# Last head group of a layer in the instruction order of the others, in a hybrid attention encoder

## The reference, cut to what matters

```
for l in range(2):
    h = rms_norm(x, g)
    z = h @ w_in[l]                      # 1024 -> 4096: qd kd vd qn kn vn gate
    # differential attention, 4 heads with two score maps each
    p = softmax(qd @ kd.T / 8 - slope * |i - j|)
    o_da = rms_norm((p[0] - lam * p[1]) @ vd, subln_g) * (1 - lam_init)
    # 2-D neighbourhood attention, 8 heads: 16 rows x 64 columns of tokens,
    # each query sees 8 rows x 16 columns of keys
    p = softmax(qn @ kn_window.T / 8 + rpb, masked)
    o_na = p @ vn_window
    x = x + (concat(o_da, o_na) * silu(gate)) @ w_out[l]
return rms_norm(x, final_g)
```

## Time and profile before

| | us |
|---|---|
| median of 3 runs | 1439.88 |
| lowest, highest | 1439.75, 1440.21 |
| the profiled execution | 1440.11 |
| its span, first to last instruction | 1438.3 |
| TensorE busy in the span | 1417.8 |
| VectorE busy | 884.0 |
| ScalarE busy | 691.5 |
| GpSimd busy | 500.2 |

### The profile page before, as it was taken

How to read it: one execution, slowest core, us unless ns; L and a number is a source line. 1 busy time by engine, 2 the same in 40 slices (tenths; PEclk the granted TensorE clock), 3 DMA queues, 4 the chain that set the end, 5 groups by cost and what they waited for, 6 DMA issues and landing times.

```text
span 1438.3 us, 23719 instructions
## 1 busy us (share of the span) xinstructions
PE 1417.8 (99%) x8116; PEld 1153.9 (80%) x8116; DVE 884.0 (61%) x1827; ACT 691.5 (48%) x1373; POOL 500.2 (35%) x416
## 2 busy tenths in 40 slices
PE   9999999999999999999999999999999999999996
PEld 7788888887888888777887888788878888887875
DVE  7767677677556565653337777767676565656433
ACT  6545554555444444552515554545544444456231
POOL 3223223233333333443643231323233333337152
PEclk9999999999999999999999999999999999999998
DMA  5710101121211111301110110100202021213113
GB/s 183 154 30 29 45 22 36 36 62 38 62 38 55 45 48 49 128 30 59 58 44 30 38 37 15 44 29 22 77 23 65 36 62 36 63 38 125 45 59 117
DMA packets 40698, 79.57 MB, mean 55 GB/s; under 512 B 18992, under 2 KB 19248, under 8 KB 40624
## 3 DMA queue, kind: packets, MB, share of 16 engines
q1 hardware_dynamic: 40480, 78.60, 17.3%
q10 hardware_dynamic: 144, 0.01, 0.0%
HBM read 66.57 MB, written 15.96 MB: 57 GB/s over the span
## 4 chain that ended last, share of the span: by engine, by line
PE 93%; DVE 3%; ACT 2%; issue 1%; DMA 1%; SPq 0%; POOL 0%; POOLq 0%; DVEq 0%; ACTq 0%
PE proj L1045 19%; PE proj L1047 18%; PE proj L1046 18%; PE scores L1081 11%; PE turn L1138 6%; PE mix L1189 3%; PE mix L1190 3%; PE mix L1154 2%; PE mix L1156 2%; PE mix L1155 2%; PE scores L1138 2%; DVE pt_lo L1554 1%; PE mix L1164 1%; DMA xt<-x_t 1%; DVE cmix L1583 1%
## 5 line engine op out<-in xcount | busy, mean ns | idle before, releaser
L1045 PE MATMUL proj<-h_hi,w_hi 128*128 128x512 f32 x1184 | 490.8, 415 | 2.0 <-DVE h_lo L1445 0.5
L1047 PE MATMUL proj<-h_hi,w_lo 128*128 128x512 f32 x1184 | 465.2, 393 | 0.0
L1046 PE MATMUL proj<-h_lo,w_hi 128*128 128x512 f32 x1184 | 462.0, 390 | 0.0
L628 POOL TENSOR_TENSOR w_lo<-w_raw,w_hi 128x1024 fp32r<-128x1024 f32 x62 | 152.8, 2464 | 486.6 <-ACT w_hi L815 486.6
L1554 DVE TENSOR_TENSOR pt_lo<-turn,pt_hi 128x512 fp32r<-128x512 f32 x208 | 139.1, 669 | 225.6 <-ACT pt_hi L857 224.9
L1047 PEld LDWEIGHTS proj<-h_hi,w_lo 128*128 128x128 f32 x1184 | 222.2, 188 | 50.6
L1045 PEld LDWEIGHTS proj<-h_hi,w_hi 128*128 128x128 f32 x1184 | 223.0, 188 | 47.9 <-issue 10.5
L1046 PEld LDWEIGHTS proj<-h_lo,w_hi 128*128 128x128 f32 x1184 | 223.8, 189 | 35.0
L857 ACT ACTIVATE pt_hi<-turn 128x512 fp32r<-128x512 f32 x208 | 120.3, 578 | 225.4 <-PE turn L1138 225.1
L1546 DVE CUSTOM_DVE_ANT_0 prob<-scores,inner 128x1024 f32<-128x1024 f32 (+1 forms) x192 | 203.5, 1060 | 3.1 <-PE scores L1081 2.7
L882 ACT ACTIVATE prob<-prob,nm,escale_now 128x1024 f32<-128x1024 f32 x128 | 158.7, 1240 | 61.6 <-DVE nm L1550 61.1
(11 more groups left out here) (187 smaller groups left out, 2274.4 us busy)
## 6 DMA issues: line engine op xcount, KB each, us to landing
w_raw<-chunks SPq DMA_DIRECT2D x80, 512.0 KB, 3.5
mixed_dram<-gate SPq DMA_DIRECT2D x28, 256.0 KB, 2.2
edge<-bias_dram SPq DMA_DIRECT2D x32, 224.0 KB, 4.8
h_lo<-mixed_dram SPq DMA_DIRECT2D x14, 512.0 KB, 6.7
xt<-x_t SPq DMA_DIRECT2D x8, 512.0 KB, 8.5
out_t<-xt SPq DMA_DIRECT2D x16, 256.0 KB, 2.1
bias_dram<-bias_rows SPq DMA_DIRECT2D x16, 240.0 KB, 6.0
dist_dram<-inner SPq DMA_DIRECT2D x1, 480.0 KB, 6.2
```

The lines of the kernel that those rows point to most:

```text
L628: pool.tensor_tensor(w_lo[:, b], w_raw[:], f32(w_hi[:, b]), ALU.subtract).then_inc(w_lo_done, 1)
L1045: pe.matmul(dst, a_hi, b_hi, start=start, stop=False)
L1046: pe.matmul(dst, a_hi, b_lo, start=False, stop=False)
L1047: return pe.matmul(dst, a_lo, b_hi, start=False, stop=stop)
```

## The change

In the last group of each layer, the scores of tile t + 1 are now computed in step t, between the two transposed parts of tile t - 1 (`following` now also answers for the last group), instead of the scores of tile t at the start of step t. On VectorE the two passes over scores (`shifted`) go to the same place as in the other groups: behind the low parts and the reciprocal, ahead of the gate piece and of the additions of the step's last slot. On ScalarE the first exponentials of a tile stand ahead of the first high part of the step, the second exponentials ahead of the second high part. The reciprocal goes behind the first low part. The other groups, and GpSimd's and SyncE's lists, are as before.

```diff
         def following(g, behind, t):


-            if not g.project:
-                return None
-            return (g, t + 1) if t < NT - 1 else (behind, 0) if t == NT - 1 else None
+            if t < NT - 1:
+                return g, t + 1
+            return (behind, 0) if t == NT - 1 and behind else None
...
-                    elif t < NT and g.project:
+                    elif t < NT:
                         exponentials(front, ft, 0)
...
-                    p_first = t == NT or not g.project
+                    p_first = t == NT
...
-                if front and ft > 1 and not g.project:
-                    score(front, ft)
...
-                if front and ft > 1 and not g.project:
-                    shift_scores(front, ft)
...
-                    if c == 0 and front and t < NT and g.project:
+                    if c == 0 and front and t < NT:
                         combine(front, ft)
...
-                if front and (t == NT or not g.project):
+                if front and t == NT:
                     combine(front, ft)
```

## The result

| | before | after |
|---|---|---|
| median, runs | 1439.82, 4 | 1453.99, 4 |
| lowest, highest | 1439.39, 1440.21 | 1453.25, 1454.39 |
| ratio of after to before | | 1.0096, 95% interval 1.0084 to 1.0108 |
| the profiled execution | 1440.11 | 1454.24 |
| its span | 1438.3 | 1452.4 |

The account below looks back on a forecast made before the run. The prediction took TensorE, 93% of the chain of waits, as the bound. New waits of 7.2 us a layer less today's 1.8 make 5.4, +10.8 us in two layers: 1450.8 us, range 1445.5 to 1454.0.

Parts of the forecast that it names:

- C: Scores of step 5, step 4's weighing, row 5 and third transpose: new TensorE waits of 0.9 and 0.3 us a layer.
- D: Bank of the first output piece: VectorE's additions later, TensorE sooner; a wait of 2.7 us a layer, upper bound 3.0.
- gain at step 4: Scores between the transposes cover TensorE's 1.61 us wait; with step 2's 0.18, at best 1.8 us a layer won.
- A: Step 2's weighing: gate piece behind both passes delays the tanh and ScalarE's queue; a wait of 1.4 us a layer.
- B: Rows 1 and 2 for the output pieces come late through GpSimd: waits of 0.65 and 1.2 us, 1.9 a layer.
- rival 4: TensorE's clock falls to 1.2 GHz behind the longest new wait, 2.1 us more a layer: 1455.0; chance 0.04.
- Its other two signs: The forecast is also wrong if VectorE's `xt` releases no TensorE wait, or if ScalarE's first tanh stays near 596.
- rival 3: The output-piece bank wait is covered and only A to C bind, 2.7 us a layer: 1445.3; chance 0.08.
- Rival 1: The gap closes and nothing else gets late, the tanh not held: 1436.3; chance 0.05.
- rival 2: Only D binds, A to C hiding behind one another; 0.9 us a layer, with 0.3 left of C: 1442.3; chance 0.07.
- rival 5: The two orders cost the same, slacks being larger than the profile tells: within 0.2%; chance 0.04.
- the rule's own price: By the skill page's find-the-gaps rule alone, the result would be the gain of 1.8 us a layer: 1436.3.

Follow-up runs that it names:

- gate_first: Changed kernel with VectorE's gate pieces put back ahead of the passes over the next scores, additions as changed: 1449.07 us, ratio 1.0064 to the kernel before.
- adds_first: Changed kernel with VectorE's additions of output pieces 0, 1 and 2 back ahead of the passes over scores: 1449.63 us, ratio 1.0066 to the kernel before.
- before_gate_late: Kernel before, with only the last group's first gate piece moved behind VectorE's passes over step 2's scores: 1447.28 us, ratio 1.0053.
- before_adds_late: Kernel before, with only the additions of output pieces 0 and 1 moved behind VectorE's passes over step 6's scores: 1449.03 us, ratio 1.0063.
- both_hi_early: both_first plus ScalarE making output chunk 2's high part ahead of its copies of the weighed pair in step 6: 1441.33 us, ratio 1.0005 to the kernel before.
- before_s5: Kernel before, with only TensorE's scores of tile 5 put between the two transposes of step 4: 1439.56 us, ratio 0.9998.
- exp_as_before: Changed kernel with ScalarE's exponentials back in the order of before: 1458.39 us, ratio 1.0133 to the kernel before.
- both_first: Changed kernel with both gate pieces and additions ahead of VectorE's passes over scores: 1444.55 us, ratio 1.0028 to the kernel before.
- before_s5_both: before_s5 plus VectorE's passes over tile 5's scores at the end of step 4, ahead of its gate scaling: 1438.91 us, ratio 0.9991 to the kernel before.
- before_hi_early: Kernel before, with only ScalarE's high part of output chunk 2's weights ahead of its copies of the weighed pair in step 6: 1439.94 us, ratio 0.9996.
- before_s5_both_hi: Kernel before with the edits of both before_s5_both and before_hi_early: 1438.97 us, ratio 0.9989.

## Why the forecast came out as it did

The result is 3.2 us above the forecast, and the sign and the main mechanism were right. That it is still inside the range, by 0.01, is luck: the 3 us above the layout's 1450.8 were given to C and D at their upper bounds, and neither went there; what used them up are a wait that was left out and a fall of the clock. By its own steps, in layer 0, as read above:

| step of the forecast | forecast | measured |
|---|---|---|
| gain at step 4 (wait of 1.61 closes) | up to 1.8 with step 2 | 1.61 to 0.14 |
| A, weighing of step 2 | 1.4 | 1.43 |
| B, row 1 | 0.65 | 0.66 |
| B, row 2 | 1.2 | 1.29 |
| C, scores of tile 5 | 0.5 | 0.30 |
| C, weighing of step 4 | 0.4 | 0.14 |
| C, row 5 and the third transpose | 0.3 | 0.42 |
| D, bank of output piece 2 | 2.7 | 2.69 |
| E, weights of output chunk 2 | none | 1.44 |
| lower clock behind D, layer 1 alone | none, rival 4 | 1.43 |

- A, B and D were right in mechanism and size, and the experiments separate them: gate_first takes A and B away and leaves D, adds_first takes VectorE's part of D and leaves A and B, before_gate_late makes A alone (its list has no wait for `h_lo`) and before_adds_late makes VectorE's part of D alone. No run makes B alone; that it comes from the gate piece rests on gate_first.
- C was 0.34 too large in all: 0.86 where 1.2 was laid out. No run takes C away or makes it alone, so its three parts rest on the timeline.
- The step that failed is the sentence "Later steps have 6.9 us and more of matmuls and stay covered". It looked at when the row copies and additions were done, and left out the weights of output chunk 2. Moving the scores takes 1.3 us of TensorE's work, from start to start, from behind each weighing, and whatever hangs on the weighing through ScalarE and GpSimd gets that much less time. At step 6 there was no slack at all. The wait is 2.9 us in two layers, 0.2 of which were there before; both_hi_early measures 3.2.
- Rival 4, given 0.04, came in part: the clock fell behind the longest new wait in one layer of two, in the profiled run, for 1.4 us, less than the 2.1 a layer that it was priced at. The forecast had named this as a sign of being wrong ("if the granted clock falls in these waits"), and by that sign this part of it was: the layout held the clock at full speed. Its other two signs did not show: `xt` releases the largest wait, and the tanh starts at 598.01.
- In the numbers: 10.8 forecast, less 0.7 for C, plus 2.7 for E (1.44 less 0.11 a layer), plus 1.4 for the clock is 14.2; the two groups are 14.6 longer and the spans differ by 14.1.
- Two slips in the working are too small to matter. D's slack was taken as 0.24, where the bank was free at 624.24 and written at 624.53, 0.29. The range was said to reach down to rival 3, whose own time, 1445.3, lies below its end of 1445.5.
- Rivals 1, 2, 3 and 5 fall. Rival 1 rested on the old gap. It closes as that rival said, and before_s5 shows that this by itself is worth nothing that the time can tell: 0.9998. The Trainium skill's page "Perfetto Trace Analysis", "Optimization Strategy", advises to find the gaps and make what they depend on start sooner. before_s5 does the first half only: it fills the gap with other work, and the low part comes no sooner (25.55 where it was 25.53). No run here makes the low part itself earlier in the old order, so the rule's own price, 1436.3, stays untried. Filling the gap gives time only with further edits that take the next waits away: 0.9991 with one and 0.9989 with two, both at the edge of what can be told.
- What the clock does is the one part not settled. By the Trainium skill's page "TensorE: Matmul & The Clock Gate", "Why this matters for your kernels", gaps between bursts cost clock; the rows agree for one layer of two and don't tell why the same wait spares the other.

## What to carry to other kernels

When work of the busiest engine moves from behind a hand-over to ahead of it, everything that hangs on that hand-over loses just so much slack: go through each chain that starts there (copies, low parts, weights, banks), not only those next to the edit, and read hidden slack from start to start of the matmuls, since a wait of 0.1 to 0.3 us has no row. On an engine that works its list in turn, put what others wait for (the subtraction that lets a tanh start, the addition that frees a bank) ahead of what is only early. A gap is worth closing only as far as the next instruction's slack goes; here a 1.6 us wait taken away alone gave 0.2 us a layer, under what the time of the kernel can tell.

## What the runs showed of the hardware that was not expected

The granted clock of TensorE fell behind a wait in one of the two layers and not in the other, though both have the same waits within 0.05 us. In the profiled runs: behind 2.53 us in layer 1 of the changed kernel, for some 3.2 us; behind 2.69 in layer 1 of before_adds_late, for some 6; behind 1.69 in layer 1 of before_gate_late, where 0.63 of waiting and two transposes stand just ahead of it; and behind 3.61 in layer 0 of exp_as_before, whose layer 1 kept full clock behind 3.62. The window of that layer 0:

```profile
631.80:634.30 2.50, 2.50 (x7) 1.88 (x6) 0.00 (x0) 0.00 (x0) 0.00 (x0) 0.50 0.02 7
```

There the first two spacings behind the wait (0.34 and 0.23, from 630.85) are those of full clock, and matmuls stand 0.43 apart only from 631.78 on, 0.9 us after TensorE has started again. The profiled run of gate_first has two waits of 2.5 us and no fall in either last group. The kernel before, with its 1.61, has none, and neither have the profiled runs of adds_first, both_first, both_hi_early, before_s5, before_s5_both, before_hi_early and before_s5_both_hi. So behind the waits of 1.69 to 3.61 us the clock took 1.4 to 2.8 us more in four of the ten last groups that have one, and nothing in the others, and single runs of one kernel differ for it: gate_first's go from 1447.07 at a mean clock of 0.996 to 1450.57 at 0.994. What decides in which layer it falls stays open.
